# Open norms spread by their own product, gate scaling on GpSimd, and suffix sums a slot later in a two-block transformer kernel

## The chip, the cores and the metric

The kernel runs on one core of a Trainium2 chip. The metric is the time of one execution on the device in microseconds (us); the median of several runs counts. "Profiled execution" is the one run that the hardware profiler recorded. Engines: TensorE (PE, with its weight loads as PEld), VectorE (DVE), ScalarE (ACT), GpSimd (POOL) and SyncE (SP), which issues the loads.

## The reference

All data is float32, one sequence of 512 tokens, model width 1024. Two blocks run one after the other.

The first block has 2 layers: a SwiGLU FFN (hidden 2816, half weight), a mixer, and another FFN. The mixer computes three kinds of attention on the normed input, weighs each with its own gate, and projects:

```
merged = g_a * (o_a @ w_br_a) + g_b * (o_b @ w_br_b) + g_c * (o_c @ w_br_c)
return merged @ w_out          # g_a, g_b, g_c: thirds of sigmoid(h @ w_gate)
```

`o_a` is stick-breaking attention with 4 heads: with z the scores, `A[t,s] = sigmoid(z_ts) * prod over s<j<t of (1 - sigmoid(z_tj))`, computed as an exponential of a suffix sum of logarithms. `o_b` is compressed, selected and windowed attention of 8 heads, `o_c` attention of 4 heads over the 256 tokens that an index scores highest.

The second block is a dilated attention, a convolution mixer and an FFN. Its mixer's and its last FFN's results are normed before they are added to x:

```
x = x + rms_norm(mixer(x), g_post_mix)
x = x + rms_norm(ffn(x), g_post_ffn)
rms_norm(x, g) = x * rsqrt(mean(x * x) + 1e-6) * g
```

## The kernel before

**Layout and loads.** x stays transposed in SBUF: 8 tiles of 128 x 512 (feature on the partitions, token in the columns). Weights arrive in units of 512 KB (128 x 1024), four buffers, issued by SyncE. ScalarE rounds a unit to its high part (`split_hi`, L299), VectorE subtracts to get the low part (`split_lo`, L304), three units ahead. TensorE makes three products of each 128 x 128 tile with 512 columns: high by high, low by high, high by low (`three`, L325 to L327). A product with `late` waits for the low part of its input tile just ahead of its use. Phases are separated by a fence of all engines.

**Norms.** `sq` is the square of a tile (ScalarE), `ssq` the sum of squares over tiles (GpSimd, L559). In an open norm nothing else can run: TensorE sums `ssq` over partitions in eight or more small products into 128x4 (token on the partition), ScalarE takes the square root (L392, behind a table load), VectorE the reciprocal (L396), four diagonal matrices are made (L399), and a product with ones spreads the value over all partitions into a PSUM bank (`spread_pe`, L384). Then VectorE multiplies each tile by the value and the gain (L2235 in block 2, L2263 at the end), and x is added, in block 2 by GpSimd (L2254), in the last FFN by VectorE for even tiles (L2267) and by GpSimd for odd ones (L2273). SyncE stores each finished tile.

**Mixer phase 2** (`mix2_*`) is ordered by hand. All engines walk over the same slots q, 20 for each block b of 128 queries (`JOBS`); in b's slots one stick-breaking head is also worked off. In a slot TensorE makes, in this order: scores of slots q and q+1 if q is even (they wait for `job_red`, VectorE's reduce of slot q-1, L1439), gate products (L618, as many as the table `GATE_FILL` has for the slot), the values' product L1102, turns, index, compressed attention, the spread of weights (L1112), and stick-breaking. The last holds the suffix sums (L1177, in slots `SUM_MADE`, waiting for `sb_lo`, VectorE's low part, L1365) and the product with v (L1183, `PV_SLOT` 19). ScalarE's slot holds the exponential of slot q-1 (L1267), the gate copy, the turn's copy (L1276), the copy of the spread weights (L1303) and then stick-breaking's step, in slot `W_SLOT` the exponential of the weights (L1237, 128x1280). VectorE reads the sums in slots `SUM_READ`.

**Mixer phase 3** (`mix3_*`) works off units "c" (gate c, finished as a product) and "branch" units (products of o_a and o_b), then the output product. The gates a and b come back by DMA (`gates_in`, issued by ScalarE, L1528), are scaled by the norm's value (`scale_ab`, L1570, 128x1024) and get their sigmoid (L1548). VectorE multiplies the branch products (L1596 ff.), adds gate c's part, ScalarE makes `m_hi` (L1552) and VectorE `m_lo` (L1604). At the phase's start VectorE also makes `o_lo` (L1581), which the first branch product needs.

Of the kernel before, what the change touches and what calls it, by code (L numbers as in the profile page):

```python
# [8 lines left out]
P = 128  # L9
# [53 lines left out]
def program(nc, A, out, layers=L, dumps=()):  # L63
# [201 lines left out]
    s = {}  # L265
    for n in ("gains_in bias_tab_in bias_mm bias_out_a bias_out_v glu qk_out o_out conv job_parts mean centred c_norm c_val c_hi c_lo ya_out x_post y_norm block_made sig_kept "
              "sq_summed stat_sum stat_std stat_rs stat_diag rstd h_f32 h_hi h_lo "
              "dve_step x_val x_hi x_lo pad sb_hi sb_lo sb_out v_out t_out turned roped small_out hid cmp_mm cmp_keys cmp_turned mixer_in zn head_sum head_std gates vcb_zero x_sent x_back gate_z ab_scaled sig_in0 sig_in1 "
              "job_red job_sc job_exp job_tr job_pv pt_out ring_in ring_out o_part gate up sig_ab rs_out xc_in split_hi split_lo coef cmp_scaled sb_z sb_sp sb_c sb_w sb_o sb_d sb_zm sb_abs sb_e sb_ln idx_acc "
              "cmp_exp cmp_sub merged_o o_hi o_lo o_tr sig branches part_sum m_val m_hi m_lo "  # L270
              "silu prod act_hi act_lo x_new sq zeroed ssq_add").split():
        s[n] = sem(n)
# [100 lines left out]
    def tile_sum_pe(pe, k, no, dst, done, squares=None):  # L373
# [39 lines left out]
    def ffn_pe(pe, f, r, post=False):  # L413
# [48 lines left out]
        if post:  # L462
            pe.wait_ge(s["ssq_add"], 2 + KD)
            stats_pe(pe, 1)

    def ffn_act(act, f, r, g=None, last=False):
# [14 lines left out]
        def down(i, final=False):  # L481
            for t in range(4):
                for j in range(3):
                    if not final or 3 * t + j + AHEAD < 12:
                        split_hi(act, rd + 3 * i, 3 * t + j + AHEAD)
                act.wait_ge(s["x_new"], 4 * i + t + 3)
                act.wait_ge(s["ssq_add"], 4 * i + t + 1)
                a = bass.ds(4 * i * S + t * S, S)
                nc.scalar.activation(sq[t % 2][:], res[:, a], ACT.Square).then_inc(s["sq"], 1)  # L489
                if not last:  # L490
                    scaled_hi(act, x[:, a], h_hi[:, a], gains[:, bass.ds(g + 4 * i + t, 1)])

        both(act, down, last)
        if last:
            stats_act(act, 1, eps_col[:, 0:1])

    def ffn_dve(dve, f, r, g=None, last=False):
# [27 lines left out]
        def down(i, final=False):  # L525
            for t in range(4):
                for j in range(3):
                    if not final or 3 * t + j + AHEAD < 12:
                        split_lo(dve, rd + 3 * i, 3 * t + j + AHEAD)
                dve.wait_ge(unit_used, SLOTS * (rd + 3 * i) + 3 * t + 3 + 1)  # L530
                a = bass.ds(4 * i * S + t * S, S)
                if last:
# [990 lines left out]
    def mix3_act(act, f, r, gn_col, l):  # L1523
# [41 lines left out]
    def mix3_dve(dve, f, r, gn_col):  # L1565

        def scale_ab(m):
            dve.wait_ge(s[f"sig_in{m % 2}"], 16 * (m // 2 + 1))
            ab = sig_ab[m % 2][:].rearrange("p (e t) -> p e t", e=2)
            nc.vector.tensor_tensor(ab, ab, rs_full[:].unsqueeze(1).to_broadcast([P, 2, S]), ALU.mult).then_inc(s["ab_scaled"], 1)  # L1570

        def gate_c(m):
# [445 lines left out]
    def blk2_pe(pe, f, r):  # L2018
# [57 lines left out]
        pe.wait_ge(s["ssq_add"], 2 * KD + 3)  # L2076
        for b in range(TB):
            nc.tensor.matmul(bank[5][:, b:b + 1], ssq[:, b * P:(b + 1) * P], inv_d, start=(b == 0), stop=False, skip_group_check=True)
        tile_sum_pe(pe, KD - 1, 2 * KD, bank[5], s["stat_sum"])
        spread_pe(pe, 1)  # L2080

    def blk2_act(act, f, r):
# [83 lines left out]
        for m in range(KD):  # L2166
# [14 lines left out]
    def blk2_dve(dve, f, r):  # L2181
# [48 lines left out]
        stats_dve(dve, 1)  # L2230
        for k in range(KD + 1):
            if k < KD:
                if k >= 2:
                    dve.wait_ge(s["x_post"], k - 1)
                nc.vector.scalar_tensor_tensor(out=val[k % 2][:], in0=tile(y_mix, k), scalar=bc("g_post_mix", k), in1=bank[6][:],  # L2235
                                               op0=ALU.mult, op1=ALU.mult).then_inc(s["y_norm"], 1)
            if k >= 1:
                g = (3 * L + 1) * KD + k - 1
                scaled_lo(dve, tile(x, k - 1), tile(h_hi, k - 1), tile(h_lo, k - 1), gains[:, g:g + 1], k)

    def blk2_pool(pool, f):
# [9 lines left out]
        pool.wait_ge(s["x_back"], 16)  # L2251
        for k in range(KD):
            pool.wait_ge(s["y_norm"], k + 1)
            nc.gpsimd.tensor_tensor(tile(x, k), tile(x, k), val[k % 2][:], ALU.add).then_inc(s["x_post"], 1)  # L2254

    def post_dve(dve):

        for k in range(KD):
            if k >= 2 and k % 2 == 0:
                dve.wait_ge(x_final, k // 2)  # L2260
            elif k >= 2:
                dve.wait_ge(x_final_pool, k // 2)
            nc.vector.scalar_tensor_tensor(out=val[k % 2][:], in0=tile(y, k), scalar=bc("g_post_ffn", k), in1=bank[6][:],  # L2263
                                           op0=ALU.mult, op1=ALU.mult).then_inc(s["y_norm"], 1)
            if k % 2 == 0:
                dve.wait_ge(s["y_norm"], k + 1)
                nc.vector.tensor_tensor(tile(x, k), tile(x, k), val[k % 2][:], ALU.add).then_inc(x_final, 1)  # L2267

    def post_pool(pool):

        for k in range(1, KD, 2):
            pool.wait_ge(s["y_norm"], k + 1)
            nc.gpsimd.tensor_tensor(tile(x, k), tile(x, k), val[k % 2][:], ALU.add).then_inc(x_final_pool, 1)  # L2273

# [4 lines left out]
    with nc.Block() as block:  # L2279
        @block.sync  # L2280
        def _(sp):
# [92 lines left out]
        def _(pool):  # L2374
# [176 lines left out]
```

## Time and profile before

| | |
|---|---|
| median of 3 runs | 3554.07 us (3553.71 to 3555.38) |
| profiled execution | 3556.05 us |
| its span | 3554.5 us |
| TensorE busy | 3493.2 us, 98% of the span |
| VectorE, ScalarE, GpSimd busy | 1942.9, 1472.2, 174.6 us |
| mean granted TensorE clock | 0.995 of full speed |
| moved by DMA | 356.06 MB, 100 GB/s |

The span is that of the profiled execution, so a sum made of its rows belongs to 3556.05, not to the median. Idle time of an engine other than TensorE costs something only where TensorE waits for it.

### The profile page before, as it was taken

The numbers are of one execution on the slowest core, as the hardware profiler recorded it, in microseconds if no ns is written. First come the engines' busy times: TensorE is split into PE (matmuls) and PEld (weight loads), VectorE is DVE, ScalarE is ACT, GpSimd is POOL, SyncE is SP. The second block draws the span as 40 slices with busy tenths as digits, with TensorE's granted clock in tenths as the row PEclk, the third lists the DMA queues.
The fourth block names the chain that finished last, engine by engine and source line by source line (L and its number), as shares of the span: only waits on it lengthen the run. The fifth ranks groups of instructions, "written<-read, shape, count | busy, mean of one in ns | idle before, by whom it ended". The sixth has DMA issues, their size and how long they took to land.

```text
span 3554.5 us, 46476 instructions
## 1 busy us (share of the span) xinstructions
PE 3493.2 (98%) x16692; PEld 2775.4 (78%) x16692; DVE 1942.9 (55%) x3249; ACT 1472.2 (41%) x2210; POOL 174.6 (5%) x181
## 2 busy tenths in 40 slices
PE   9999999999999999999999999999999999999997
PEld 7888886667888888888866578888887777878886
DVE  5443466767544344434657675443378776645433
ACT  5432355654444234423456544442233434434421
POOL 0000000000000000000000001000000001020001
PEclk9999999999999999999999999999999999999999
DMA  4233422114322332235221053223422223313231
GB/s 142 95 100 105 158 98 72 42 58 159 139 94 100 102 101 95 94 105 164 91 80 54 28 172 139 94 95 106 141 95 83 78 75 104 116 62 104 96 105 65
DMA packets 99831, 356.06 MB, mean 100 GB/s; under 512 B 11823, under 2 KB 12079, under 8 KB 98920
## 3 DMA queue, kind: packets, MB, share of 16 engines
q1 hardware_dynamic: 83232, 300.16, 25.2%
q10 hardware_dynamic: 9416, 30.34, 2.6%
q0 software_dynamic: 7040, 23.66, 1.8%
q8 instruction: 89, 1.46, 0.2%
q14 instruction: 54, 0.44, 0.0%
HBM read 330.98 MB, written 26.80 MB: 101 GB/s over the span
## 4 chain that ended last, share of the span: by engine, by line
PE 89%; DVE 6%; ACT 3%; issue 2%; POOLq 0%; DMA 0%; POOL 0%; ACTq 0%; DVEq 0%; SPq 0%
PE bank L325 25%; PE bank L327 24%; PE bank L326 24%; PE bank L618 5%; PE bank L1102 1%; PE bank L1073 1%; PE bank L1748 1%; PE bank L1082 1%; DVE unit_lo L304 1%; PE bank L1721 1%; ACT unit_hi L299 1%; PE bank L1177 1%; PE bank L1737 1%; PE bank L1119 1%; PE bank L1164 1%
## 5 line engine op out<-in xcount | busy, mean ns | idle before, releaser
L304 DVE TENSOR_TENSOR unit_lo<-unit_raw,unit_hi 128x1024 fp32r<-128x1024 f32 x526 | 647.4, 1233 | 693.0 <-ACT unit_hi L299 682.6
L325 PE MATMUL bank<-h_hi,unit_hi 128*128 128x512 f32 x2416 | 956.2, 396 | 5.7 <-DVE h_lo L409 4.1
L327 PE MATMUL bank<-h_hi,unit_lo 128*128 128x512 f32 x2416 | 943.1, 390 | 0.0
L326 PE MATMUL bank<-h_lo,unit_hi 128*128 128x512 f32 x2416 | 942.6, 390 | 0.0
L299 ACT ACTIVATE unit_hi<-unit_raw 128x1024 fp32r<-128x1024 f32 x526 | 552.9, 1053 | 355.2 <-PE bank L327 342.6
L325 PEld LDWEIGHTS bank<-h_hi,unit_hi 128*128 128x128 f32 x2416 | 455.0, 188 | 115.3 <-issue 22.1
L327 PEld LDWEIGHTS bank<-h_hi,unit_lo 128*128 128x128 f32 x2416 | 454.7, 188 | 96.5
L326 PEld LDWEIGHTS bank<-h_lo,unit_hi 128*128 128x128 f32 x2416 | 455.2, 188 | 92.8 <-issue 1.7
L325 PE MATMUL bank<-act_hi,unit_hi 128*128 128x512 f32 x880 | 346.7, 394 | 0.0
L327 PE MATMUL bank<-act_hi,unit_lo 128*128 128x512 f32 x880 | 345.0, 392 | 0.0
L326 PE MATMUL bank<-act_lo,unit_hi 128*128 128x512 f32 x880 | 341.5, 388 | 0.0
L477 ACT ACTIVATE act_hi<-val 128x512 f32 x110 | 69.6, 633 | 459.9 <-DVE val L518 459.9
L327 PEld LDWEIGHTS bank<-act_hi,unit_lo 128*128 128x128 f32 x880 | 165.2, 188 | 38.7
L326 PEld LDWEIGHTS bank<-act_lo,unit_hi 128*128 128x128 f32 x880 | 165.2, 188 | 37.0
L325 PEld LDWEIGHTS bank<-act_hi,unit_hi 128*128 128x128 f32 x880 | 165.4, 188 | 32.9
L559 POOL TENSOR_TENSOR ssq<-ssq,sq 128x512 f32<-128x512 f32 x64 | 84.7, 1323 | 1971.6 <-ACT sq L489 1718.4
L1899 DVE SCALAR_TENSOR_TENSOR val<-u_conv,block_columns,val 128x512 f32<-128x512 f32 x232 | 174.1, 750 | 6.4 <-DVE neg_m L1955 0.3
L516 DVE TENSOR_TENSOR val<-silu,bank 128x512 f32<-128x512 f32 x110 | 75.6, 687 | 153.2 <-PE bank L327 153.2
L474 ACT ACTIVATE silu<-silu 128x512 f32<-128x512 f32 x110 | 69.6, 633 | 205.1 <-DVE silu L512 205.1
L325 PE MATMUL bank<-unit_hi,h_hi 128*128 128x512 f32 x352 | 143.1, 407 | 0.0
L327 PE MATMUL bank<-unit_hi,h_lo 128*128 128x512 f32 x352 | 137.5, 391 | 0.0
L326 PE MATMUL bank<-unit_lo,h_hi 128*128 128x512 f32 x352 | 137.2, 390 | 0.0
(325 smaller groups left out, 4540.9 us busy)
## 6 DMA issues: line engine op xcount, KB each, us to landing
unit_raw<-in_units SPq DMA_DIRECT2D x564, 512.0 KB, 3.3
gates_kept<-gate_z POOLq DMA_DIRECT2D x32, 256.0 KB, 2.3
sig_ab<-gates_kept ACTq DMA_DIRECT2D x16, 512.0 KB, 3.6
bias_rows<-bias_once POOLq DMA_DIRECT2D x2, 3840.0 KB, 20.7
x_kept<-x ACTq DMA_DIRECT2D x3, 2048.0 KB, 11.0
x<-x_kept ACTq DMA_DIRECT2D x3, 2048.0 KB, 8.6
xc<-xc ACTq DMA_DIRECT2D x16, 256.0 KB, 4.4
bias_t<-bias_rows POOLq DMA_DIRECT2D x16, 256.0 KB, 3.7
```

Source lines behind the costliest of these rows:

```text
L299: nc.scalar.activation(w_hi[u % SLOTS][:], raw[u % SLOTS][:], ACT.Copy).then_inc(unit_hi, 1)
L304: nc.vector.tensor_tensor(w_lo[u % SLOTS][:], raw[u % SLOTS][:], w_hi[u % SLOTS][:].bitcast(F32), ALU.subtract).then_inc(unit_lo, 1)
L325: nc.tensor.matmul(out_ap, w_h, r_h, start=first, stop=False)
L326: nc.tensor.matmul(out_ap, w_h, r_l, start=False, stop=False)
L327: return nc.tensor.matmul(out_ap, w_l, r_h, start=False, stop=last)
L474: nc.scalar.activation(silu[t][:], silu[t][:], ACT.Silu).then_inc(s["silu"], 1)
L477: nc.scalar.activation(act_hi[:, bass.ds(2 * i * S + t * S, S)], val[t][:], ACT.Copy).then_inc(s["act_hi"], 1)
L516: nc.vector.tensor_tensor(val[t][:], silu[t][:], bank[2 + t][:], ALU.mult).then_inc(s["up"], 1)
L559: nc.gpsimd.tensor_tensor(ssq[:], ssq[:], sq[m % 2][:], ALU.add).then_inc(s["ssq_add"], 1)
L618: mm = nc.tensor.matmul(bank[7][:], w[:, k], tile(h, i // 3), start=(i == 0), stop=(i == 23), skip_group_check=True)
L1073: mm = nc.tensor.matmul(bank[a % 2][:, 0:(b + 1) * P], q, k, start=(part == 0), stop=(part == 2))
L1899: ins = nc.vector.scalar_tensor_tensor(out=dst, in0=u_conv[:, u0 + k:u0 + k + S], scalar=w, in1=val[0][:], op0=ALU.mult, op1=ALU.add)
```

## The change

1. `mean_square_pe`, `root_act`, `reciprocal_dve` (both open norms of block 2): two products of the matrix `inv_d_sq` (128x128, all 1/1024) with `ssq` over the first seven tiles and with the last `sq` give the mean square already spread over all partitions; root and reciprocal work on 128x512 in SBUF. The small products, the diagonal and the spread product go. In the last FFN ScalarE squares the last tile straight from the bank.
2. Block 2: tile 0's x addition moves from GpSimd to VectorE.
3. End: the eight multiplications run in place behind each other, GpSimd adds x to tiles 0 to 4, VectorE to 5 to 7.
4. Mixer phase 2: the sums are made and read a slot later, the weights' exponential in slot 18; the gate fill is rearranged.
5. Mixer phase 3: `scale_ab` moves from VectorE to GpSimd; in branch units the split of the next weight unit moves ahead of `m_hi` and `m_lo`.

```
+    def mean_square_pe(pe, dst, squares):
+        nc.tensor.matmul(dst[:], inv_d_sq, ssq[:], start=True, stop=False)
+        pe.wait_ge(s["sq"], squares)
+        nc.tensor.matmul(dst[:], inv_d_sq, sq[(KD - 1) % 2][:], start=False, stop=True).then_inc(s["stat_sum"], 1)
+    def root_act(act, std, sums):
+        act.wait_ge(s["stat_sum"], 2)
+        nc.scalar.activation(std[:], sums[:], ACT.Sqrt, bias=eps_col[:, 0:1]).then_inc(s["stat_std"], 1)
+    def reciprocal_dve(dve, rs, std):
+        dve.wait_ge(s["stat_std"], 2)
+        nc.vector.reciprocal(rs[:], std[:]).then_inc(s["stat_rs"], 1)
+        dve.wait_ge(s["stat_rs"], 2)
...
-            pe.wait_ge(s["ssq_add"], 2 + KD)
-            stats_pe(pe, 1)
+            pe.wait_ge(s["ssq_add"], 2 + KD - 1)
+            mean_square_pe(pe, bank[7], KD)
...
-    Z_MADE, Z_READ, SUM_MADE, SUM_READ = (0, 2, 4), (1, 3, 5), (11, 13, 15), (12, 14, 16)
-    EXP_SLOT, LN_SLOT, SP_SLOT, LO_SLOT, W_SLOT, PV_SLOT, OUT_SLOT = 6, 8, 9, 10, 17, 19, 19
+    Z_MADE, Z_READ, SUM_MADE, SUM_READ = (0, 2, 4), (1, 3, 5), (12, 14, 16), (13, 15, 17)
+    EXP_SLOT, LN_SLOT, SP_SLOT, LO_SLOT, W_SLOT, PV_SLOT, OUT_SLOT = 6, 8, 9, 10, 18, 19, 19
...
-    GATE_FILL = ((7, 5, 7, 6, 9, 2, 10, 8, 6, 10, 6, 4, 4, 7, 8, 4, 5, 7, 7, 0),
-                 (7, 3, 3, 2, 8, 10, 1, 8, 7, 9, 4, 4, 3, 7, 4, 2, 2, 6, 5, 0),
-                 (2, 9, 0, 2, 4, 10, 8, 6, 6, 6, 3, 2, 1, 3, 2, 0, 0, 1, 4, 0),
-                 (1, 6, 0, 0, 3, 4, 7, 6, 3, 6, 0, 2, 0, 3, 3, 5, 3, 6, 0, 0),
+    GATE_FILL = ((7, 5, 7, 6, 9, 2, 10, 8, 6, 10, 6, 8, 2, 10, 4, 5, 3, 7, 7, 0),
+                 (7, 3, 3, 2, 8, 10, 1, 8, 7, 9, 4, 8, 0, 10, 1, 1, 1, 6, 5, 0),
+                 (2, 10, 0, 2, 4, 10, 8, 6, 6, 6, 3, 3, 0, 6, 0, 0, 0, 0, 4, 0),
+                 (1, 6, 0, 0, 3, 4, 7, 6, 3, 6, 0, 2, 0, 6, 0, 6, 2, 6, 0, 0),
...
 # mix3_act, branch unit; mix3_dve alike with split_lo and m_lo
-            split_hi(act, r, u + AHEAD)
+            if u == 0 or MERGE_ORDER[u - 1][0] == "c":
+                split_hi(act, r, u + AHEAD)
...
+            if u + 1 < MERGE_UNITS:
+                split_hi(act, r, u + 1 + AHEAD)
             act.wait_ge(s["m_val"], m + 1)
             nc.scalar.activation(tile(m_hi, m), val[0][:], ACT.Copy).then_inc(s["m_hi"], 1)
...
     def mix3_pool(pool, f):
         fence(pool, f)
+        for m in range(KD):
+            pool.wait_ge(s[f"sig_in{m % 2}"], 16 * (m // 2 + 1))
+            ab = sig_ab[m % 2][:].rearrange("p (e t) -> p e t", e=2)
+            nc.gpsimd.tensor_tensor(ab, ab, rs_full[:].unsqueeze(1).to_broadcast([P, 2, S]), ALU.mult).then_inc(s["ab_scaled"], 1)
...
+            if k == 0:
+                dve.wait_ge(s["x_back"], 16)
+                dve.wait_ge(s["y_norm"], 1)
+                nc.vector.tensor_tensor(tile(x, 0), tile(x, 0), val[0][:], ALU.add).then_inc(s["x_first"], 1)
...
+    POST_POOL, POST_ORDER = 5, (0, 1, 2, 3, 5, 6, 4, 7)
...
-            nc.vector.scalar_tensor_tensor(out=val[k % 2][:], in0=tile(y, k), scalar=bc("g_post_ffn", k), in1=bank[6][:],
+            nc.vector.scalar_tensor_tensor(out=tile(y, k), in0=tile(y, k), scalar=bc("g_post_ffn", k), in1=silu[1][:],
```

## Rows read from the trace of the kernel before

**Rows 1.** The page: busy time of each engine, share of the span, instructions.
```profile
PE 3493.2 (98%) x16692; PEld 2775.4 (78%) x16692; DVE 1942.9 (55%) x3249; ACT 1472.2 (41%) x2210; POOL 174.6 (5%) x181
```
**Rows 2.** Waits of TensorE: what for, us in total, times, longest.
```profile
PE bank L1177 <- DVE sb_lo L1365: 10.0, 8, 1.8
PE bank L325 <- DVE m_lo L1604: 6.7, 4, 1.7
```
**Rows 3.** Windows: us, busy of PE, PEld, DVE, ACT, POOL, clock, DMA share, GB/s.
```profile
742.10:745.50 3.40, 3.40 (x15) 2.35 (x15) 1.61 (x4) 0.82 (x2) 0.00 (x0) 0.53 0.20 77
850.00:860.00 10.00, 10.00 (x45) 8.19 (x45) 7.58 (x11) 4.12 (x5) 0.00 (x0) 1.00 0.45 147
```
**Rows 4.** Timeline, last head of a layer, slot 11 to 12: start, us, instruction.
```profile
741.38 0.68 DVE L1439 CUSTOM_DVE_ANT_0 sq<-bank,mixer_constants 128x512 f32<-128x512 f32 x1
741.51 0.50 PE L1177 MATMUL bank<-val_r,tri_r 128*128 128x512 f32 x1 [1.77 <-DVE sb_lo L1365]
```
**Rows 5.** Lines by form, the reduce at 128 columns.
```profile
L1439 DVE CUSTOM_DVE_ANT_0 sq<-bank,mixer_constants 128x128 f32<-128x128 f32 x40 | 11.1, 288 | 32.7 <-PE bank L1073 31.2 <-ACT prob L1267 1.5
```
**Rows 6.** Timeline, first head of a layer, slots 17 to 19.
```profile
581.34 1.28 ACT L1237 ACTIVATE sb_z<-sb_z 128x1280 f32<-128x1280 f32 x1
584.14 0.60 ACT L1303 ACTIVATE spread_c<-bank 128x512 f32<-128x512 f32 x1 [0.20 <-PE bank L1112]
584.45 1.99 PE L1183 MATMUL bank<-sb_z,v_nat 128*128 128x512 f32 x5
```
**Rows 7.** Timeline, last head of a layer, slots 18 to 19.
```profile
765.12 0.60 ACT L1303 ACTIVATE spread_c<-bank 128x512 f32<-128x512 f32 x1 [0.16 <-PE bank L1112]
765.93 1.89 PE L1183 MATMUL bank<-sb_z,v_nat 128*128 128x512 f32 x5
```
**Rows 8.** Timeline, end of mixer phase 3.
```profile
858.22 0.37 ACTq L1528 DMA_DIRECT2D sig_ab<-gates_kept  x1
859.49 1.22 DVE L1570 TENSOR_TENSOR sig_ab<-sig_ab,rstd_full 128x1024 f32<-128x1024 f32 x1
867.06 0.50 PE L325 MATMUL bank<-m_hi,unit_hi 128*128 128x512 f32 x1 [1.72 <-DVE m_lo L1604]
```
**Rows 9.** Lines by form, GpSimd's addition of 512 columns.
```profile
L1327 POOL TENSOR_TENSOR o_t<-o_t,part_o 128x512 f32<-128x512 f32 x16 | 20.4, 1277 | 120.2 <-DVE part_o L1424 80.3 <-ACT o_t L1297 20.8 <-issue 19.0
```
**Rows 10.** Timeline, from the last product to the last addition.
```profile
3533.52 0.69 DVE L533 COPY y<-bank 128x512 f32<-128x512 f32 x1 [14.42 <-PE bank L327]
3534.24 0.63 ACT L489 ACTIVATE sq<-y 128x512 f32<-128x512 f32 x1 [14.48 <-DVE y L533]
3534.89 1.28 ACT L392 ACT_TABLE_LOAD   x1
3540.91 0.75 DVE L2263 SCALAR_TENSOR_TENSOR val<-y,block_columns,bank 128x512 f32<-128x512 f32 x1 [2.17 <-PE bank L384]
3543.12 1.26 POOL L2273 TENSOR_TENSOR x<-x,val 128x512 f32<-128x512 f32 x1 [6.91 <-DVE val L2263]
3543.73 1.20 DVE L2267 TENSOR_TENSOR x<-x,val 128x512 f32<-128x512 f32 x1
3550.77 1.26 POOL L2273 TENSOR_TENSOR x<-x,val 128x512 f32<-128x512 f32 x1 [1.29 <-DVE val L2263]
```
**Rows 11.** Timeline, start of mixer phase 3.
```profile
787.84 3.70 DVE L1581 TENSOR_TENSOR o_lo<-o_t,o_hi 128x512 fp32r<-128x512 f32 x6
793.67 0.40 PE L325 MATMUL bank<-o_hi,unit_hi 128*128 128x512 f32 x1
```
**Rows 12.** Lines by form, reciprocals.
```profile
L1930 DVE RECIPROCAL rden<-den 128x1 f32<-128x1 f32 x32 | 5.0, 157 | 6.0 <-PE bank L1748 6.0
L1406 DVE RECIPROCAL coef<-den 128x8 f32<-128x8 f32 x16 | 3.2, 198 | 0.2
```
**Rows 13.** Timeline, open norm of the block-2 mixer.
```profile
3152.34 0.27 ACT L392 ACTIVATE norm_small<-bank,eps_col 128x4 f32<-128x4 f32 x1
3159.97 0.77 PE L325 MATMUL bank<-h_hi,unit_hi 128*128 128x512 f32 x1 [4.11 <-DVE h_lo L409]
```

More of the change, by code:

```diff
@@ L265, in program @@
     s = {}
[L266 removed]
+    for n in ("gains_in bias_tab_in bias_mm bias_out_a bias_out_v glu qk_out o_out conv job_parts mean centred c_norm c_val c_hi c_lo ya_out x_post x_first y_norm block_made sig_kept "
               "sq_summed stat_sum stat_std stat_rs stat_diag rstd h_f32 h_hi h_lo "
@@ L485, in down @@
                         split_hi(act, rd + 3 * i, 3 * t + j + AHEAD)
-                act.wait_ge(s["x_new"], 4 * i + t + 3)
+                a = bass.ds(4 * i * S + t * S, S)
+                if final and t == 3:
+                    act.wait_ge(unit_used, SLOTS * (rd + 3 * i) + 3 * t + 3 + 1)
+                else:
+                    act.wait_ge(s["x_new"], 4 * i + t + 3)
                 act.wait_ge(s["ssq_add"], 4 * i + t + 1)
-                a = bass.ds(4 * i * S + t * S, S)
-                nc.scalar.activation(sq[t % 2][:], res[:, a], ACT.Square).then_inc(s["sq"], 1)
+                nc.scalar.activation(sq[t % 2][:], bank[4 + t % 2][:] if final and t == 3 else res[:, a], ACT.Square).then_inc(s["sq"], 1)
                 if not last:
@@ L494, in ffn_act @@
         if last:
-            stats_act(act, 1, eps_col[:, 0:1])
+            root_act(act, silu[0], bank[7])
     def ffn_dve(dve, f, r, g=None, last=False):
@@ L530, in down @@
                 dve.wait_ge(unit_used, SLOTS * (rd + 3 * i) + 3 * t + 3 + 1)
+                if final and t == 3:
+                    dve.wait_ge(s["sq"], KD)
                 a = bass.ds(4 * i * S + t * S, S)
@@ L542, in ffn_dve, with ffn_pool @@
         if last:
-            stats_dve(dve, 1)
+            reciprocal_dve(dve, silu[1], silu[0])
             post_dve(dve)
-    def ffn_pool(pool, f, l=None):
+    def ffn_pool(pool, f, l=None, last=False):
         fence(pool, f)
@@ L551, in ffn_pool, with sum_squares @@
         nc.gpsimd.memset(ssq[:], 0.0).then_inc(s["ssq_add"], 2)
-        sum_squares(pool)
-    def sum_squares(pool, use=0):
-        for m in range(KD):
+        sum_squares(pool, n=KD - 1 if last else KD)
+    def sum_squares(pool, use=0, n=KD):
+        for m in range(n):
             pool.wait_ge(s["sq"], KD * use + m + 1)
@@ L2076, in blk2_pe @@
         pe.wait_ge(s["ssq_add"], 2 * KD + 3)
[L2077 to L2080, printed above, removed]
+        mean_square_pe(pe, bank[5], 2 * KD)
     def blk2_act(act, f, r):
@@ L2173, in blk2_act @@
             nc.scalar.activation(sq[m % 2][:], tile(y_mix, m), ACT.Square).then_inc(s["sq"], 1)
-        stats_act(act, 1, eps_col[:, 0:1], bank[5])
+        root_act(act, part2_[0], bank[5])
         for k in range(KD):
-            act.wait_ge(s["x_post"], k + 1)
+            act.wait_ge(s["x_first" if k == 0 else "x_post"], max(k, 1))
             g = (3 * L + 1) * KD + k
@@ L2229, in blk2_dve @@
             nc.vector.tensor_copy(tile(y_mix, m), bank[6 + m % 2][:]).then_inc(s["x_new"], 1)
-        stats_dve(dve, 1)
+        reciprocal_dve(dve, part2_[1], part2_[0])
         for k in range(KD + 1):
             if k < KD:
-                if k >= 2:
-                    dve.wait_ge(s["x_post"], k - 1)
-                nc.vector.scalar_tensor_tensor(out=val[k % 2][:], in0=tile(y_mix, k), scalar=bc("g_post_mix", k), in1=bank[6][:],
+                if k == 2:
+                    dve.wait_ge(s["x_first"], 1)
+                if k >= 3:
+                    dve.wait_ge(s["x_post"], k - 2)
+                nc.vector.scalar_tensor_tensor(out=val[k % 2][:], in0=tile(y_mix, k), scalar=bc("g_post_mix", k), in1=part2_[1][:],
                                                op0=ALU.mult, op1=ALU.mult).then_inc(s["y_norm"], 1)
+            if k == 0:
+                dve.wait_ge(s["x_back"], 16)
+                dve.wait_ge(s["y_norm"], 1)
+                nc.vector.tensor_tensor(tile(x, 0), tile(x, 0), val[0][:], ALU.add).then_inc(s["x_first"], 1)
             if k >= 1:
@@ L2251, in blk2_pool @@
         pool.wait_ge(s["x_back"], 16)
[L2252 removed]
+        for k in range(1, KD):
             pool.wait_ge(s["y_norm"], k + 1)
             nc.gpsimd.tensor_tensor(tile(x, k), tile(x, k), val[k % 2][:], ALU.add).then_inc(s["x_post"], 1)
+    POST_POOL, POST_ORDER = 5, (0, 1, 2, 3, 5, 6, 4, 7)
     def post_dve(dve):
         for k in range(KD):
[L2259 to L2262, printed above, removed]
[L2263 removed]
+            nc.vector.scalar_tensor_tensor(out=tile(y, k), in0=tile(y, k), scalar=bc("g_post_ffn", k), in1=silu[1][:],
                                            op0=ALU.mult, op1=ALU.mult).then_inc(s["y_norm"], 1)
[L2265 to L2267 removed]
+        for k in range(POST_POOL, KD):
+            dve.wait_ge(s["y_norm"], k + 1)
+            nc.vector.tensor_tensor(tile(x, k), tile(x, k), tile(y, k), ALU.add).then_inc(x_final, 1)
     def post_pool(pool):
[L2271 removed]
+        for k in range(POST_POOL):
             pool.wait_ge(s["y_norm"], k + 1)
[L2273 removed]
+            nc.gpsimd.tensor_tensor(tile(x, k), tile(x, k), tile(y, k), ALU.add).then_inc(x_final_pool, 1)
     PER_LAYER, PHASES = 51, 5
@@ L2293, in _ @@
                     sp.dma_start(raw[q][:], A["units"][SLOTS * r + q]).then_inc(raw_full[q], 16)
-            for k in range(KD):
-                if k % 2 == 0:
-                    sp.wait_ge(x_final, k // 2 + 1)
+            for k in POST_ORDER:
+                if k < POST_POOL:
+                    sp.wait_ge(x_final_pool, k + 1)
                 else:
-                    sp.wait_ge(x_final_pool, k // 2 + 1)
+                    sp.wait_ge(x_final, k - POST_POOL + 1)
                 sp.dma_start(out[:, k * S:(k + 1) * S], tile(x, k)).then_inc(stored, 16)
@@ L2384, in _ @@
             blk2_pool(pool, F2 + 1)
-            ffn_pool(pool, F2 + 2)
+            ffn_pool(pool, F2 + 2, last=True)
             post_pool(pool)
```

13 lines of the change are left out of this document (4 added, 9 removed).

## The prediction

> **What bounds the kernel now.** I read the page first: TensorE is busy in 98% of the span and VectorE in 55%, ScalarE in 41% [rows 1]. So TensorE's stream sets the time, and only what makes it stand, slows its clock or lengthens the few serial stretches can move the sum. The list of what TensorE waits for is short [rows 2]: the two entries that the edits aim at are the sums of stick-breaking (10.0 us in 8 waits, one per head and layer) and the late half of the merged tile in mixer phase 3 (6.7 us in 4). Even if both vanished the kernel would gain 16.7 us, 0.5%. Then the windows [rows 3]: in dense work 45 products take 10.00 us, 0.22 us each, at a granted clock of 1.00, the 2.4 GHz level; right after the longest stick-breaking wait there is a stretch of 3.40 us at 0.53, the 1.2 GHz level. Half of it, 1.7 us, is loss. I put one such stretch in each layer.
>
> The profiled execution took 3556.05 us (span 3554.5, 1.55 around it), 1.98 above the median of 3554.07. I sum against 3556.05 and subtract 2 at the end.
>
> **1. Sums one slot later, mixer phase 2.** The sums of a head leave slots 11, 13, 15 for 12, 14, 16. Their low parts are then ready, so the 10.0 us go. But TensorE's slot 12 opens with scores that wait for VectorE's reduce of slot 11, and that reduce stands on VectorE right behind the low part: in the last head the sums start at 741.51 and the reduce runs from 741.38 to 742.06 [rows 4]. It takes 0.68 us at 512 columns and 0.28 at 128 [rows 5]. The wait so moves from the low part to the reduce and grows by about 0.2, 0.33, 0.46 and 0.6 us for heads 0 to 3, 1.6 a layer. Against it stand the gate products that the new fill table puts ahead of it: 4, 4, 1 and 0 more in slot 11, 9 x 0.23 = 2.1 us of cover. Over two layers 3.2 − 4.1 = −0.9. Bounds: all cover lost, +3.2; the reduce ready in time, −10.0. The total number of gate products stays; a few gate units end a slot earlier or later, and with them ScalarE's gate copy and the transfer on GpSimd's queue, behind which nothing urgent stands there: nothing for that.
>
> **2. The weights' exponential, slot 17 to 18.** The product with v (L1183) stays in slot 19. In ScalarE's slot 18 the exponential stands behind the copy of the spread weights, which itself waits for TensorE's spread products. In the first head the copy starts at 584.14, takes 0.60, the exponential 1.28 [rows 6]; so it runs 584.65 to 585.93, where L1183 started at 584.45: TensorE stands 1.5 us. In the last head the copy starts at 765.12, the exponential would end at 766.9, and L1183 started at 765.93 [rows 7]: 1.0 us, as a turn lies between. Slot 19 holds no gate products in either table, so nothing else covers it. Two heads at 1.5 and two at 1.0, twice: +10.0. Lower bound 0 (were the copy early), upper +12. It was covered before by a whole slot.
>
> **Clock.** A new idle of some 1.5 us per head, and a wait of 1.77 + 0.6 us in the last, can bring further half-speed stretches; one costs 1.7 [rows 3]. Bounds −3.4 (none left) and +7 (four more). One idle of 1.77 us in the last head did it; the other six waits of [rows 2] average 1.1 (10.0 less 2 x 1.77, by 6) and I saw no such stretch behind them; 1.5 lies between. I take +2.
>
> **3. Mixer phase 3: scaling on GpSimd, splits earlier.** At the end TensorE waits for the merged tile's low part, 1.72 us at 867.06. VectorE's queue ahead of it held the scaling of the last gate pair, 1.22 us at 859.49 [rows 8]. With it gone and the weight split ahead of the high part, both waits per layer would close: −6.7. But the pair lands 3.6 us after its transfer's issue at 858.22 and GpSimd then needs two times 1.28 us for 1024 columns (from a 512-column addition [rows 9]): about 861.5 to 864. That is where VectorE makes the two products of the tile. The tail shows the pair side by side: GpSimd's addition runs 3543.12 to 3544.38, VectorE's, begun at 3543.73, takes 1.20, and ends 0.55 after it [rows 10], against 0.69 for a copy of that size [rows 10]. So VectorE stands through GpSimd's instruction, and I give back one of two waits per layer: −3.3.
>
> The Trainium skill (SBUF — State Buffer, Who interferes with whom) says that a VectorE instruction with two SBUF inputs and a GpSimd one share a port which the first starter keeps to its end. The trace agrees, by the 1.20 of [rows 10].
>
> At its start GpSimd scales pairs 0 and 1 while VectorE makes o_lo, 3.70 us in six at 787.84, of which the first branch product at 793.67 needs the last [rows 11]. Two scalings of 2.55 us hold VectorE 5.1 us at most; slack there is 793.67 − 791.54 = 2.1. So 0 to +3.4 a layer; I take the middle, +1.7, +3.4 for both. GpSimd's queue holds nothing else until the sums of squares behind the phase, and the earlier weight splits free their buffers, so SyncE's loads start, up to a microsecond earlier: with the DMA engines 0.45 busy there [rows 3], nothing for that. The phase comes to 0.1, bounds −6.7 and +3.5.
>
> **4. The reciprocal at 128x512.** Twice a reciprocal of 128x4 becomes one of 128x512. 128x1 takes 157 ns, 128x8 198 ns [rows 12], 5.9 ns a column: 3.2 us. The small forms here can't decide that.
>
> **5. Norm after the block-2 mixer.** The small square root starts at 3152.34, just behind its table load; a 128x512 one starts there too, 0.6, then 3.2: 3156.2, where the spread product's end opened the old chain (4.11 before 3159.97 [rows 13], 3155.86). The first addition moves from GpSimd (1.25) to VectorE (0.7), but the second GpSimd addition, begun just before VectorE's first low part, holds that up. First product at 3160.5 for 3159.97: +0.5. Bounds −3 (fast reciprocal, free port) and +2.
>
> **6. The tail.** Squaring from the bank starts with the last product's end, 3533.52, the copy's 0.72 earlier; then 0.63, table load 1.28, square root 0.62, reciprocal 3.2: 3539.35, for 3540.91 now [rows 10]: −1.5. Behind it stand eight products of 0.75, three VectorE additions and five GpSimd additions of 1.26, all on SBUF now. Six VectorE instructions free (0.74) and five each behind a GpSimd one (1.26 + 0.55 less 0.1 of overhead): 4.4 + 8.5 = 12.9, end 3552.2. Before, the last addition ended at 3550.77 + 1.26 = 3552.03. So 0. Bounds: port free, 8.1 us of VectorE alone and the rest hidden, −5; GpSimd starved to the end, +1.
>
> **Sum.** −0.9 + 10.0 + 2.0 + 0.1 + 0.5 + 0 = +11.7: 3567.7 on the profiled execution, 3565.7 by the median. That is the forecast.
>
> **Rivals.**
> *A free port.* GpSimd and VectorE don't hinder each other: the phase-3 start costs 0, both waits close (−6.7), the tail gives −5, term 5 −0.5: 11.7 − 0.1 − 6.7 − 5 − 1 = −1.1, 3553. For it: [rows 10] is one collision, and the two products of the merged tile read a bank, not two SBUF tiles. Against: that row's 1.20. It decides against me once two of the three places are free. Chance 0.17. This is the case that ends not slower.
> *The exponential is covered.* TensorE comes to L1183 late enough or the copy early, and half or less of term 2 appears: 3555 to 3561, point 3558. For it: a wait of TensorE lets VectorE catch up, so the next slots' waits [rows 2] may pay back. Against: in [rows 6, 7] the copy follows TensorE's own spread products, so both move together. Chance 0.17; half of it within 0.2%.
> *The change doesn't move the sums' wait*, or gives all of it back: the reduce is early, term 1 is −10.0, no slow stretch is left, −3.4 for +2: 3551. Against: in [rows 4] the reduce only starts when the low part ends. Chance 0.08.
> *More slow stretches and a stalled start* of phase 3: +7 for +2, +3.5 more: 3573, or above. The idles of 1.5 us lie near the 1.77 that did it [rows 4]. Chance 0.13.
> *My forecast,* 3560 to 3569: 0.45.
>
> **Numbers.** This kernel's measurement tells 0.2%, 7.1 us, from no change. Faster needs under 3547: only the first and third rival with a fast reciprocal (−5.0 over both) reach it, 0.14. Within 0.2%: the rest of these and most of the second, 0.26. Slower: forecast, the last rival and the rest, 0.60. Range 3549 to 3574; the forecast's own 3560 to 3569.
>
> **What would show it.** In the list of waits, L1177's line should fall away, and a wait of the scores for the reduce appear, 8 times, about 9 us; L1183 waits for ScalarE's L1237, 8 times, 10 us; m_lo's line halves. The reciprocals show 3.2 us, the tail's VectorE products and additions alternate with GpSimd's at 1.2 or more. I am wrong if L1183 starts with no idle ahead, or if the tail closes by 3548.

## The result

The changed kernel is slower. Its median is 3569.61 us (3565.66 to 3571.49, 6 runs) for 3554.72 (3553.59 to 3557.1, 6 runs): ratio 1.0038, 95% interval 1.0028 to 1.0048. I had forecast 3565.7, in a range of 3549 to 3574. The profiled execution took 3565.66 us, its span 3564.1. That is 9.6 above the profiled one of before, while the medians lie 14.9 apart; the rest is in the clock, below.

The page's busy times of the changed kernel, which answer to [rows 1]:

```profile
PE 3485.7 (98%) x16672; PEld 2771.5 (78%) x16672; DVE 1966.9 (55%) x3225; ACT 1473.3 (41%) x2210; POOL 215.4 (6%) x196
```

TensorE was busy 7.5 us less and the span grew by 9.6, so it stood some 17 us longer, a part of that where the norms' small products were. TensorE's list of waits in the changed kernel, as in [rows 2] (what for, us in total, times, longest):

```profile
PE bank L1093 <- DVE neg_m L1459: 9.1, 6, 2.4
PE bank L1203 <- ACT sb_z L1257: 9.0, 8, 1.4
PE bank L325 <- DVE h_lo L424: 8.6, 1, 8.6
PE bank L325 <- DVE unit_lo L304: 7.7, 3, 3.3
...
PE bank L325 <- DVE m_lo L1623: 4.2, 2, 2.2
```

The sums' wait for the low part is gone and the scores' wait for the reduce stands in its place, 9.1 for 10.0. L1203 is the product with v (L1183 before): 9.0 us where none was. The late tile's wait fell from 6.7 to 4.2. Of the 7.7 us for a weight's low part 6.6 are new, two waits at the start of phase 3, where VectorE makes that low part behind `o_lo`.

The first head, slots 17 to 19, timeline of the changed kernel; it answers to [rows 6]:

```profile
582.79 0.60 ACT L1323 ACTIVATE spread_c<-bank 128x512 f32<-128x512 f32 x1 [1.35 <-PE bank L1132]
583.28 1.26 ACT L1257 ACTIVATE sb_z<-sb_z 128x1280 f32<-128x1280 f32 x1
584.60 2.20 PE L1203 MATMUL bank<-sb_z,v_nat 128*128 128x512 f32 x6 [1.42 <-ACT sb_z L1257]
```

The exponential (L1257) starts when the copy (L1323) is done, and TensorE idles 1.42 us for it. ScalarE itself had idled 1.35 us ahead of the copy, where the exponential could have run. In heads 2 and 3 the wait is 0.84.

The last head, slot 11 to 12, changed kernel, to [rows 4]:

```profile
742.86 0.42 DVE L1385 TENSOR_TENSOR sb_lo<-sb_a,cmp_r 128x256 fp32r<-128x256 f32 x1
743.19 0.68 DVE L1459 CUSTOM_DVE_ANT_0 sq<-bank,mixer_constants 128x512 f32<-128x512 f32 x1
743.94 0.80 PE L1093 MATMUL bank<-qk_hi 64*128 64x512 f32 x2 [2.39 <-DVE neg_m L1459]
```

Low part, then reduce, then the scores: 2.39 us of idle for 1.77.

Phase 3, its start and its end in the first layer, changed kernel, to [rows 11] and [rows 8]:

```profile
790.86 8.11 DVE L1599 TENSOR_TENSOR o_lo<-o_t,o_hi 128x512 fp32r<-128x512 f32 x6
791.58 5.64 POOL L1639 TENSOR_TENSOR sig_ab<-sig_ab,rstd_full 128x1024 f32<-128x1024 f32 x2 [14.08 <-DMA sig_ab<-gates_kept]
800.16 0.51 PE L325 MATMUL bank<-o_hi,unit_hi 128*128 128x512 f32 x1 [3.33 <-DVE unit_lo L304]
...
868.08 2.40 POOL L1639 TENSOR_TENSOR sig_ab<-sig_ab,rstd_full 128x1024 f32<-128x1024 f32 x1 [8.70 <-DMA sig_ab<-gates_kept]
868.37 2.65 DVE L1617 TENSOR_TENSOR part<-part,part 128x512 f32<-128x512 f32 x1
871.06 0.69 DVE L1619 TENSOR_TENSOR val<-part,sig_c 128x512 f32<-128x512 f32 x1
871.67 1.22 DVE L304 TENSOR_TENSOR unit_lo<-unit_raw,unit_hi 128x1024 fp32r<-128x1024 f32 x1
872.81 0.69 DVE L1623 TENSOR_TENSOR m_lo<-val,m_hi 128x512 fp32r<-128x512 f32 x1
```

The six subtractions of o_lo took 8.11 us for 3.70: they stood through both of GpSimd's scalings. At the end an addition of 0.69 us took 2.65, to 871.02, beside the last scaling's 868.08 to 870.48. The unit's split, now between `val` and the low part, adds its 1.22.

The norm after the block-2 mixer, changed kernel, to [rows 13]:

```profile
3161.02 0.69 ACT L390 ACTIVATE part<-bank,eps_col 128x512 f32<-128x512 f32 x1
3161.74 3.35 DVE L394 RECIPROCAL part<-part 128x512 f32<-128x512 f32 x1 [2.69 <-ACT part L390]
3167.46 1.83 DVE L424 SCALAR_TENSOR_TENSOR h_lo<-x,gains,h_hi 128x512 fp32r<-128x512 f32 x1
3167.48 1.26 POOL L2278 TENSOR_TENSOR x<-x,val 128x512 f32<-128x512 f32 x1 [11.83 <-DVE val L2255]
3169.44 0.76 PE L325 MATMUL bank<-h_hi,unit_hi 128*128 128x512 f32 x1 [8.55 <-DVE h_lo L424]
```

The reciprocal takes 3.35 us, and the first low part, 1.83 us, stands through GpSimd's addition. And the tail, changed kernel, to [rows 10]:

```profile
3545.18 3.35 DVE L394 RECIPROCAL silu<-silu 128x512 f32<-128x512 f32 x1 [1.24 <-ACT silu L390]
3548.56 10.41 DVE L2285 SCALAR_TENSOR_TENSOR y<-y,block_columns,silu 128x512 f32<-128x512 f32 x8
3549.39 8.37 POOL L2295 TENSOR_TENSOR x<-x,y 128x512 f32<-128x512 f32 x5 [19.22 <-DVE y L2285]
3558.90 1.88 DVE L2289 TENSOR_TENSOR x<-x,y 128x512 f32<-128x512 f32 x3
```

Eight multiplications of 0.75 take 10.41 us, 1.3 each, while GpSimd adds; the last addition ends at 3560.78.

### The profile page after: what moved, and what is told of

It reads as the page before. It is cut to its first block, busy times and chain, and to the rows that moved or that the text cites. A ratio compares the mean times of both kernels' runs of the same rounds, so it can differ in the third digit from the quotient of the medians.

```text
span 3564.1 us, 46423 instructions
## 1 busy us (share of the span) xinstructions
PE 3485.7 (98%) x16672; PEld 2771.5 (78%) x16672; DVE 1966.9 (55%) x3225; ACT 1473.3 (41%) x2210; POOL 215.4 (6%) x196
## 4 chain that ended last, share of the span: by engine, by line
PE 92%; DVE 4%; ACT 2%; issue 1%; DMA 0%; POOLq 0%; DVEq 0%; ACTq 0%; SPq 0%
PE bank L325 26%; PE bank L327 26%; PE bank L326 25%; PE bank L638 5%; PE bank L1122 1%; PE bank L1093 1%; PE bank L1769 1%; PE bank L1102 1%; PE bank L1742 1%; PE bank L1197 1%; PE bank L1758 1%; PE bank L1139 1%; PE bank L1184 1%; PE bank L1203 1%; DVE unit_lo L304 0%
## 5 line engine op out<-in xcount | busy, mean ns | idle before, releaser
L304 DVE TENSOR_TENSOR unit_lo<-unit_raw,unit_hi 128x1024 fp32r<-128x1024 f32 x526 | 659.9, 1257 | 691.1 <-ACT unit_hi L299 680.8
```

The costliest lines, as they stand in the source:

```text
L304: nc.vector.tensor_tensor(w_lo[u % SLOTS][:], raw[u % SLOTS][:], w_hi[u % SLOTS][:].bitcast(F32), ALU.subtract).then_inc(unit_lo, 1)
```

## The experiments

Each ran on the same chip as runs of the kernel before; the difference given is to those runs' median. The first four take the mixer's phase 2 apart.

**Only the mixer's part.** The kernel before with `SUM_MADE`, `SUM_READ`, `W_SLOT` and `GATE_FILL` of the change.

> Only the mixer's part of the change: sums made and read a slot later, the weights' exponential in slot 18, the new gate fill. My account: the stall ahead of the product with v is 4.5 us a layer, the sums' wait only falls from 5.0 to 4.5, and gate products in fewer, longer runs give back some 2 us a layer; with one slow clock stretch more that is +5.3 us, 3560. Rival, that the sum of the mixer's waits is all there is (nothing given back): +8.1 and a stretch, 3564.

Measured 3559.63 us for 3555.84, ratio 1.0008 (0.9999 to 1.0018), +3.8, at the edge of what can be told from no change. Waits as named: 9.0 for the exponential, 9.0 for the reduce. My account's 3560 holds, the rival's 3564 doesn't: the highest of eleven runs is 3560.82.

**Only the gate fill.**

```
-    GATE_FILL = ((7, 5, 7, 6, 9, 2, 10, 8, 6, 10, 6, 4, 4, 7, 8, 4, 5, 7, 7, 0),
+    GATE_FILL = ((7, 5, 7, 6, 9, 2, 10, 8, 6, 10, 6, 8, 2, 10, 4, 5, 3, 7, 7, 0),
...
```

> Only the new gate fill table, sums and exponential in their old slots. My account: slot 11 has 4, 4, 1 and 0 more gate products ahead of the sums, so their wait falls by 0.75, 0.92, 0.23 and 0 us, 1.9 a layer, and the denser runs give 2 us a layer: -7.8, 3546. Rival: the products taken out of slots 12 to 17 covered other waits, which come up instead, and the total is 0 or above.

Measured 3549.93, ratio 0.9983 (0.9974 to 0.9992), −5.9: faster than the kernel before, by 1.9 less than expected. Its waits:

```profile
PE bank L1177 <- DVE sb_lo L1365: 6.2, 6, 1.8
```

3.8 us less, as worked out. A wait of the values' product for the turn's copy (0.66 us, once a layer) came up, which is the rival's mechanism at 1.3 us. And the denser runs gave less than the 2 us a layer that I had put down: in the second layer, with one slow stretch of the clock in both traces, TensorE's busy time in phase 2 fell by 0.9 us.

**Only the slots, old fill.**

```
-    Z_MADE, Z_READ, SUM_MADE, SUM_READ = (0, 2, 4), (1, 3, 5), (11, 13, 15), (12, 14, 16)
-    EXP_SLOT, LN_SLOT, SP_SLOT, LO_SLOT, W_SLOT, PV_SLOT, OUT_SLOT = 6, 8, 9, 10, 17, 19, 19
+    Z_MADE, Z_READ, SUM_MADE, SUM_READ = (0, 2, 4), (1, 3, 5), (12, 14, 16), (13, 15, 17)
+    EXP_SLOT, LN_SLOT, SP_SLOT, LO_SLOT, W_SLOT, PV_SLOT, OUT_SLOT = 6, 8, 9, 10, 18, 19, 19
```

> Only the later slots, with the old gate fill table. My account: product with v stalls 4.5 us a layer, the scores wait for the reduce without the new cover, 6.6 us a layer for 5.0: +12.2 and a slow stretch or two, 3567 to 3570. Rival, that the fill table does nothing but cover: 2.1 us a layer less than this from the other side, that is e1 plus 4.

Measured 3565.59, ratio 1.0029 (1.0016 to 1.0041), +9.8. The reduce costs 13.4 us of waits in 8, the exponential 9.0:

```profile
PE bank L1073 <- DVE neg_m L1439: 13.4, 8, 2.4
PE bank L1183 <- ACT sb_z L1237: 9.0, 8, 1.4
```

A little under my 3567. It lies 6.0 above the run with the new fill, 4.4 of it in the first of these rows. So the later slots are the loss in this phase and the fill table is a gain, with them or without.

**The exponential ahead of the copy.** The mixer's part, and in ScalarE's slot:

```
+            if b < TB and at == W_SLOT:
+                stick(b, at)
             if spread(q):
...
-            if b < TB:
+            if b < TB and at != W_SLOT:
                 stick(b, at)
```

> The mixer's part, with the weights' exponential ahead of the copy of the spread weights in ScalarE's slot 18. My account: the exponential is then done long before slot 19 and the 9.0 us of waits of the product with v go; the copy comes 1.28 us later, for which only VectorE's merge waits. e1 less 9, 3550. Rival: the copy's delay holds the next merge, exponentials and turns, and half or more of the 9 us comes back as another wait of TensorE.

Measured 3551.81, ratio 0.9988 (0.9979 to 0.9997), −4.0, so 7.8 below the mixer's part for 9.0 expected. ScalarE's timeline in slot 18:

```profile
581.62 1.27 ACT L1237 ACTIVATE sb_z<-sb_z 128x1280 f32<-128x1280 f32 x1
583.08 0.60 ACT L1305 ACTIVATE spread_c<-bank 128x512 f32<-128x512 f32 x1 [0.19 <-PE bank L1112]
```

The exponential fits into the idle time ahead of the copy, and the copy isn't even late. Two waits of 0.39 us are left. The product's wait fell from 9.0 us to 0.8 by the order on ScalarE alone.

The next four take phase 3 and the norms apart.

**Only phase 3.** The kernel before with the changed `mix3_act`, `mix3_dve`, `mix3_pool`.

> Only mixer phase 3's part: gate scaling on GpSimd, split of the next unit ahead of the merged tile's high and low part. My account: two scalings stand beside o_lo and stall TensorE 3.3 us at the phase's start, the last one stands beside an addition of the last tile and leaves one wait of 2.0 to 2.2 where two of 1.7 were: +1.9 a layer, +3.8, 3559. Rival, that the changed kernel's start waits came from the mixer's later end and not from GpSimd: then only the late waits change, -2.5, 3553.

Measured 3564.21 for 3555.57, ratio 1.0024 (1.0014 to 1.0033), +8.6. The waits are those of my account: the start's two waits of 3.3 us stand here too, with phase 2 untouched, so the rival falls. But the expected 3559 was missed by 5 us: the price is twice the 4.1 us that the waits come to. The first start wait lasts from 793.8 to 797.1, and at 796.0 a slow stretch begins (window: us, busy of PE, PEld, DVE, ACT, POOL, clock, DMA share, GB/s):

```profile
796.00:802.80 6.80, 5.70 (x13) 4.46 (x14) 4.61 (x5) 2.09 (x3) 0.00 (x0) 0.50 0.49 156
```

6.8 us at the 1.2 GHz level, and further such stretches of 3.4 us at 874.5 (behind the late wait) and 2062.3 (in the last moment of the second layer's start wait). None of them is in the trace of the kernel before. TensorE works at half speed in 12.3 us of these 13.6, the rest lies in the waits, which costs it some 6 us. With the waits that makes 10.3 for the 9.3 us by which the profiled spans differ. All ten runs of this kernel show a mean granted clock of 0.992 to 0.994, the 32 of the kernel before beside them 0.994 to 0.996.

**Only the split order.** Scaling stays on VectorE; splits as in the change (`split_hi` and `split_lo` of unit u + 1 ahead of `m_hi` and `m_lo`).

> Only the split order of phase 3; the scaling stays on VectorE. My account: VectorE's work ahead of the last tile's low part is the same, only its order changes; the first late wait grows by the split's 1.2 us and the second shrinks by it: 0, 3555. Rival, the order is what opens the late waits: -3 to -6.7, 3550.

Measured 3556.22, ratio 1.0002 (0.9993 to 1.0011). In one layer, by TensorE's waits, the first late wait grew from 1.72 to 1.96 and the second stayed at 1.65, in the other only one of 1.96 was left. Order alone gives nothing that can be measured, as expected, though the first wait grew by less than I said.

**GpSimd behind o_lo, gates fetched earlier.** Phase 3's part, and

```
+        pool.wait_ge(s["o_lo"], KD)
         for m in range(KD):
...
+            if m + 2 < KD:
+                act.wait_ge(s["branches"], m + 1)
+                gates_in(m + 2)
             act.wait_ge(s["m_val"], m + 1)
             nc.scalar.activation(tile(m_hi, m), val[0][:], ACT.Copy).then_inc(s["m_hi"], 1)
-            if m + 2 < KD:
-                gates_in(m + 2)
```

> The phase-3 part, but GpSimd waits for o_lo before it scales, and each gate pair's transfer is issued as soon as the products that read its buffer are done, 1.5 us earlier. My account (a shared port that GpSimd holds for its whole instruction): the 3.3 us at the start go, and the last scaling ends 1.4 us earlier, so 0.6 us of the 2.0 stay: 6.7 + 2.8 below e5, 3549. Rival (GpSimd's load on SBUF slows VectorE wherever they run side by side): the start's stall moves to the next instructions and at most 2 us come back.

Measured 3549.23, ratio 0.9982 (0.9973 to 0.9991), −6.3: 15.0 below phase 3 as changed, for 9.5 expected; the mean granted clock is 0.994 to 0.996 again. Start and end:

```profile
789.44 3.69 DVE L1580 TENSOR_TENSOR o_lo<-o_t,o_hi 128x512 fp32r<-128x512 f32 x6
793.22 6.68 POOL L1621 TENSOR_TENSOR sig_ab<-sig_ab,rstd_full 128x1024 f32<-128x1024 f32 x2 [17.12 <-DVE o_lo L1580]
795.27 2.35 DVE L304 TENSOR_TENSOR unit_lo<-unit_raw,unit_hi 128x1024 fp32r<-128x1024 f32 x1 [1.00 <-ACT unit_hi L299]
797.55 0.68 DVE L1573 TENSOR_TENSOR sig_c<-bank,rstd_full 128x512 f32<-128x512 f32 x1
...
861.63 2.43 POOL L1621 TENSOR_TENSOR sig_ab<-sig_ab,rstd_full 128x1024 f32<-128x1024 f32 x1 [8.71 <-DMA sig_ab<-gates_kept]
...
862.68 0.68 DVE L1596 TENSOR_TENSOR sig_c<-sig_c,bank 128x512 f32<-128x512 f32 x1
863.40 1.22 DVE L1598 TENSOR_TENSOR part<-part,part 128x512 f32<-128x512 f32 x1
```

o_lo takes its 3.69 us again, and TensorE has no wait there any more. The stall itself does move, to the next VectorE instruction with two SBUF inputs beside GpSimd, a weight split of 2.35 us for 1.22, but that one has the time. The instruction behind it, with one input in a bank, takes its usual 0.68 beside GpSimd. That is the port account and not the rival's, by which every instruction would slow down. The run has two edits at once; the waits tell them apart: the two at the start (6.6 us) are gone by the first, and of the 4.2 us of the late ones 1.0 are left with the second. At the end three instructions with one input in a bank run beside GpSimd at 0.68 or 0.69, and only the one with two SBUF inputs stands, to 864.62, until GpSimd is through at 864.06. One late wait of 0.5 us a layer is left.

**Only the norms.**

> Only the two open norms and the order behind them. My account: block 2's first product 0.8 us later, one slow clock stretch of 13.7 us is 10.2, -1.7, the tail to the last addition -0.3 and the last store 0.8 later: -0.4, 3555. Rival, that the norms carry the rest of what the changed kernel lost beyond my forecast: +2 to +4, 3558.

Measured 3556.70, ratio 1.0004 (0.9995 to 1.0013), +1.1; between the two accounts (3555 and 3558), and not to be told from no change.

**The norm's value in a bank.** The norms' part, and

```
-            reciprocal_dve(dve, silu[1], silu[0])
+            reciprocal_dve(dve, bank[6], silu[0])
...
-scalar=bc("g_post_ffn", k), in1=silu[1][:],
+scalar=bc("g_post_ffn", k), in1=bank[6][:],
```

in both norms.

> Only the norms' part, as in the run of it alone, but the reciprocal is written to a PSUM bank, from where the multiplications read it. My account: in the tail the eight multiplications (12.2 us with the additions, each 1.3) no longer wait for GpSimd's additions and take 0.76 each; GpSimd's five end 7.2 us after the first one's start, VectorE's first addition waits for the last of them, all is done after 9.1: -3.1 against the norms alone, 3553.6. Rival, that the 1.3 us is the multiplication's own time at this form of operands: no change, 3556.7.

Measured 3552.82 for 3555.47, ratio 0.9994 (0.9985 to 1.0003), −2.7 and 3.8 below the norms alone. Its tail:

```profile
3538.43 5.36 DVE L2284 SCALAR_TENSOR_TENSOR y<-y,block_columns,bank 128x512 f32<-128x512 f32 x8
3539.26 6.61 POOL L2294 TENSOR_TENSOR x<-x,y 128x512 f32<-128x512 f32 x5 [19.23 <-DVE y L2284]
3543.71 3.32 DVE L2288 TENSOR_TENSOR x<-x,y 128x512 f32<-128x512 f32 x3
```

Eight multiplications in 5.36 us where they took 10.4, with GpSimd adding from the second on.

**The tail without GpSimd.** The norms' part with `POST_POOL, POST_ORDER = 0, (0, 1, 2, 3, 4, 5, 6, 7)`.

> The norms' part alone, with all eight x additions of the tail on VectorE and none on GpSimd. Shared port: 8 x 0.75 + 8 x 0.70 = 11.6 us for the 12.2 with GpSimd's help, so nothing is lost by doing without it: -0.6, 3556. Rival, the engines run side by side: five additions more on VectorE cost 3.5, 3560.

Measured 3554.82, ratio 1.0001 (0.9992 to 1.0010), 1.8 below the norms alone:

```profile
3539.96 5.39 DVE L2284 SCALAR_TENSOR_TENSOR y<-y,block_columns,silu 128x512 f32<-128x512 f32 x8
3545.27 4.90 DVE L2288 TENSOR_TENSOR x<-x,y 128x512 f32<-128x512 f32 x8
```

VectorE does all sixteen in 10.2 us, where I had expected 11.6; with GpSimd's five additions the same work took 12.2. By the traces the help costs 2 us.

**The change, repaired.** All of the change, with the three repairs (exponential ahead of the copy, GpSimd behind o_lo and the early fetch, value in a bank).

> The whole change as made, with only the named faults taken out: weights' exponential ahead of the copy, GpSimd behind o_lo and the early gate transfer, the norm's value in a bank. If my account of the loss is whole: 3569.6 - 7.8 - 15.0 - 3.1 = 3543.7. Rival, something of the loss lies elsewhere: above 3550.

Measured 3542.93, ratio 0.9966 (0.9955 to 0.9978). The three repairs take 26.7 us off the changed kernel's 3569.61, to within 1 us of the 3543.7 that my account gave; nothing of the loss is left over.

**The best of both.** As above, but sums and exponential in their old slots, with the new fill.

> Sums and exponential in their old slots with the new gate fill, phase 3 with GpSimd behind o_lo and the early gate transfer, norms with their value in a bank. If the parts add: -5.9, -6.3 and -2.0 against before, 3541.5. Rival, the parts share a slack or the clock takes some of it back: half of it, 3548.

Measured 3539.53, ratio 0.9959 (0.9945 to 0.9973): 15.9 us faster than the kernel before, and the parts add. This is the version that beats both.

## Why the prediction was right, and where its terms were off

The forecast, slower by about 12, came out, at 14.9 by the medians. The largest new wait is the one named, 9.0 us for the exponential behind the copy. But the sum was right in part by luck: it put 11.1 us into the mixer's phase 2 (steps 1, 2 and the clock), 0.1 into phase 3 and 0.5 into the norms, and the runs of each part alone show +3.8, +8.6 and +1.1 by their medians, each with an interval of some 3 us to either side. So by these runs phase 3 carries the larger part of the loss. By the forecast's own steps, against the profiled executions:

| step | forecast | trace |
|---|---|---|
| 1 sums a slot later | −0.9 | −0.9 |
| 2 exponential behind the copy | +10.0 | +9.0 |
| clock | +2.0 | 0: one stretch more in the mixer, +1.7, one less in block 2, −1.7 |
| 3 phase 3 | +0.1 | +4.1 |
| 5 norm in block 2 | +0.5 | +0.8 |
| 6 tail | 0 | +0.6: −0.3 to the last addition, last store 0.8 later |
| not foreseen: TensorE's products in the mixer | | −4.6 |
| sum | +11.7 | +9.0, of 9.6 measured |

**Steps 1 and 2** had mechanism, place and nearly size; the run with the exponential ahead of the copy shows step 2, the two runs that part slots from fill show step 1. It was 1.42 and 0.84 us a head for 1.5 and 1.0.

**Step 3** is the term that was mis-sized. The mechanism was named, but of 0 to 3.4 at the start I took the middle. The trace had no ground for a middle: all six o_lo subtractions have two SBUF inputs and run while both transfers land. 5.1 us of scaling less 2.1 of slack is 3.0 a layer (the 3.4 written there doesn't follow from these two); the two scalings took 5.64 us, and the wait was 3.33. The Trainium skill (SBUF — State Buffer, Who interferes with whom) calls the ports that the two engines share an exclusive lock, and so points at this end. The trace agrees with it, by 8.11 for 3.70 us. At the end the wait fell by 1.25 us a layer, not 1.65, and for another reason than I gave: the tile's products with one input in a bank, at which I had put the collision, take 0.68 us beside GpSimd, and it is the addition behind them, with both inputs in SBUF, that stood 2 us; the split came ahead of the low part besides. And what the waits bring in slow clock, some 6 us in the run of phase 3 alone, stood in no term of this step.

**Step 4**, 3.2 us for the reciprocal, measured 3.35. The Trainium skill (VectorE: DVE Perf Modes, Walkthrough: the 8-slice pipeline in each mode) names a repeat count of 8 for the reciprocal. That this means eight cycles for each element was my reading, and the estimate of 4.3 us rests on it; the measurement decides against it for this form.

**Step 6** came out by two errors that cancel: VectorE alone is faster than I took it (0.61 to 0.67 an instruction back to back), and each collision costs more.

**The clock.** Between the profiled executions it costs nothing net, but the changed kernel's profiled one was the fastest of its six, with a mean granted clock of 0.995; the other five show 0.993 or 0.994. One stretch of 3.4 us at half takes 1.7 us and 0.0005 off that mean, so by these rounded figures they hold some two to four more, 3 to 7 us. Of the 5.3 us between 9.6 and 14.9, 4.0 are this, the median above the profiled execution; the other 1.3 are that the kernel before had its profiled one above its median. Where the stretches of those five lie was not recorded. The run of phase 3 alone makes its new waits the likely place: there the clock is low in all ten runs, and with most of the waits taken away it is not. My +2 was put in phase 2; by this the larger share belongs to phase 3.

**Not foreseen: the products themselves.** I held the number of gate products for the whole cost. In the second layer, with the same 3.4 us of slow clock in both, TensorE's busy time from the first gate product of phase 2 to its last product fell from 255.2 us (1777.2 to 2042.4) to 252.9 (1781.9 to 2048.8). How it divides among the kinds is less sure, since the ends of products are modelled: by ends, gate products fell by 2.2 and index products by 1.0; by the start of the next product, gates fell by 1.4, sums by 1.3 and index products by 1.1, while the turns rose by 1.5. Counted there by ends: a gate product behind another advances the stream by 0.23 us (333 of them before, 338 after), one behind a score product by 0.43 (34, then 30), one behind a sum product by 0.28. The changed kernel's timeline shows the first two kinds:

```profile
562.02 0.30 PE L1093 MATMUL bank<-qk_hi,qk_lo 64*128 64x128 f32 x2
562.25 0.50 PE L638 MATMUL bank<-h_hi,unit_hi 128*128 128x512 f32 x1
562.59 0.40 PE L638 MATMUL bank<-h_lo,unit_hi 128*128 128x512 f32 x1
...
565.55 0.39 PE L638 MATMUL bank<-h_hi,unit_hi 128*128 128x512 f32 x1
565.78 0.39 PE L638 MATMUL bank<-h_lo,unit_hi 128*128 128x512 f32 x1
```

From start to start, 562.25 to 562.59 is 0.34 where 565.55 to 565.78 is 0.23. By ends again, the fill alone took 1.0 us off the gate products there, the slots alone 1.1. Four fewer behind score products, at 0.20 more each, are 0.8 us of the 2.2. Where the rest comes from, why a change of kind costs this, and why the index products fell with the slots, no run tried; it stays open.

So the forecast was nearer than its terms: +4 in phase 3 and some 5 of clock were missed, −4.6 in the products was missed too, and the misses nearly cancel. One slip changes nothing else: the fourth rival's terms add up to 3574, not 3573.

## What to carry to other kernels

Before moving a step on one engine by a slot, write down what stands ahead of it in that engine's slot and whether that waits for the very engine that will need the step: here 1.26 us of exponential behind a 0.6 us copy cost 9 us of waits in eight places, with 1.35 us of idle time just ahead. Work handed to GpSimd was not free here where VectorE had instructions with two SBUF inputs at the same time (8.11 us for 3.70); put one input in a bank, or hold GpSimd back until that stretch is over. Price a new wait by more than its length: here 4.1 us of waits came with some 6 us of half-speed clock. A bound whose mechanism is known and whose place is crowded is to be taken at its end, not in the middle.

## What the runs showed of the hardware that was not expected

- GpSimd's additions beside VectorE's made both together slower than VectorE alone: 12.2 us for 10.2.
- A VectorE instruction with one input in PSUM was not held by GpSimd's: 0.67 us a multiplication beside five GpSimd additions, 1.3 with both inputs in SBUF.
- A reciprocal of 128x512 took 3.35 us, into SBUF or into a bank (3.36).
- A wait of 3.3 us brought 6.8 us at the 1.2 GHz level in one execution of phase 3's part and none there in the execution of the whole change that was profiled; in the changed kernel's profile a wait of 1.6 us at 681.5 has one behind it, and the same wait of the second layer, at 1945.8, has none. The times of one kernel go with its mean clock: of the 32 runs of the kernel before beside the phase-3 runs, the eight at 0.994 took 3556.4 to 3558.1 us, the 23 at 0.995 3553.3 to 3556.6.
